# Fourteen modulation vectors of a two-model transformer kernel formed on VectorE instead of TensorE

## The chip, the cores and the metric

The kernel runs on one core of a Trainium2 chip. The metric is the device time of one execution in microseconds; the figure to be predicted is the median of several runs.

## The reference

Two small transformer models are evaluated one after the other on 256 tokens of width 1024 (the second model on 256 tokens and 256 context tokens). Each sub-layer normalises the residual stream, scales and shifts it, applies a mixer or a gated feed-forward network, and adds the result back under a gate. What matters here is where scale, shift and gate come from:

```python
mod = (jax.nn.silu(c) @ ada_w[layer] + ada_b[layer]).reshape(B, 3, 3, D)
h = modulate_pre(x, g[0, 0], mod[:, 0, 0], mod[:, 0, 1])
y = swiglu_ffn(h, ffn_w_in[layer, 0], ffn_w_out[layer, 0])
x = gated_post_add(x, y, g[0, 1], mod[:, 0, 2], 0.5)
...
shift, scale = jnp.split(jax.nn.silu(c) @ kv_ada_w + kv_ada_b, 2, axis=-1)
```

Each of these vectors is one product of a conditioning vector of 1024 numbers with a 1024 x 1024 block of a weight matrix: 4 MB of fp32 are read and each is used once. There are 32 of them, in fp32 throughout.

## The kernel before, in words

**Sub-layers.** `subs` holds eleven sub-layers, in this order: 0 feed-forward, 1 short convolution, 2 feed-forward, 3 the shared keys and values ("kv"), 4 feed-forward, 5 sparse attention ("nsa"), 6 feed-forward, then 7 to 10 of the second model. The change concerns 0, 2 and 4. Between 56 and 271 us of the profile lies sub-layer 0, between 281 and 403 sub-layer 1, between 412 and 626 sub-layer 2, from 636 on kv, between 709 and 926 sub-layer 4, and between 935 and 1111 nsa.

**A feed-forward sub-layer** with 256 tokens has eleven up steps and eleven down steps. Every weight comes in units of 1 MB (128 x 2048 fp32) into `stage`, a ring of three. ScalarE rounds a unit to `w_hi` (L689), VectorE subtracts to get `w_lo` (L1074), both rings of three, and TensorE forms hi x hi, lo x hi and hi x lo. An up step j uses two units, each with 48 matmuls of 128x256 (L1653 to L1655), in two halves q of 24. A down step uses one unit in 24 matmuls of 128x512 (L1705), 12 for each of two token tiles. Up steps run as one straight block of three, a hardware loop over two more such blocks, and steps 9 and 10; down steps run as three straight steps, a loop over two blocks of three, and two more. In the last two down steps the order is tile 0 with both units, then tile 1 with both.

**Between two sub-layers** (`boundary`) VectorE first splits the next sub-layer's first unit (`split(nu)`), and then, tile after tile, updates the residual stream (`y_update`, L1134, L1143) and normalises it (`x_norm`, up to L1157); TensorE transposes each tile (L1664), VectorE applies scale and shift (L1169), ScalarE and GpSimd split the result. TensorE's next matmuls wait for that.

**A modulation vector on TensorE.** Its 4 MB come in four units into `ada`, a ring of two, on the same in-order queue (SyncE's) as the weights. `vec_acc` (L1628) takes two of the units: 16 matmuls, with the conditioning column as the stationary operand and 512 columns of the unit moving; after both halves VectorE copies the row (`vec_row`, L1087), `vec_sum` (L1639, 4 matmuls that stand as 8 records) turns it into a column form, and `vec_col` (L1100) adds the bias. The semaphores `ada_used`, `ada_rowed`, `ada_sum` and `ada_col` count units, rows, sums and columns. In a feed-forward sub-layer each block of three up steps makes one vector (a half ahead of its first step, a half ahead of its second, the sum at its end), steps 9 and 10 and the first down step make two more: five for each of sub-layers 0, 2 and 4. The first half of the first vector of sub-layers 1 and 2 is placed into the boundary ahead of them (`fills`). In nsa five vectors are made in ten halves, at every second one of its jobs J = 2, 4 ... 20 (`nsa_vec`), among the attention's matmuls.

## Time and profile before

| | |
|---|---|
| median of three runs | 2375.61 us (2375.02 to 2376.76) |
| the profiled execution, its own time | 2372.45 us |
| its span in the trace | 2370.4 us |
| TensorE busy | 2208.2 us, 93% |
| VectorE busy | 1173.6 us, 50% |
| ScalarE busy | 931.5 us, 39% |
| GpSimd busy | 99.8 us, 4% |
| read from HBM | 408.47 MB, 173 GB/s over the span |

PE is TensorE's matmul row and PEld its weight loads, which overlap; DVE is VectorE, ACT ScalarE, POOL GpSimd. Matmuls are pipelined: the duration of one (0.28 us for 256 columns) is longer than the distance from one start to the next, and it is the distance that counts. An fp32 matmul stands as several records.

### The profile page before, as it was taken

The numbers are of one execution on the slowest core, as the hardware profiler recorded it, in microseconds if no ns is written. First come the engines' busy times: TensorE is split into PE (matmuls) and PEld (weight loads), VectorE is DVE, ScalarE is ACT, GpSimd is POOL, SyncE is SP. The second block draws the span as 40 slices with busy tenths as digits, with TensorE's granted clock in tenths as the row PEclk, the third lists the DMA queues.
The fourth block names the chain that finished last, engine by engine and source line by source line (L and its number), as shares of the span: only waits on it lengthen the run. The fifth ranks groups of instructions, "written<-read, shape, count | busy, mean of one in ns | idle before, by whom it ended". The sixth has DMA issues, their size and how long they took to land.

```text
span 2370.4 us, 35346 instructions
## 1 busy us (share of the span) xinstructions
PE 2208.2 (93%) x14350; PEld 1886.1 (80%) x14350; DVE 1173.6 (50%) x1973; ACT 931.5 (39%) x1376; POOL 99.8 (4%) x156
## 2 busy tenths in 40 slices
PE   4999998999889998998999899888999999898999
PEld 1898786998788977766998898566778768777997
DVE  2444556444634446464445663865222233865454
ACT  2333424333533335444335543654222122554343
POOL 2000000000100000011000100001000000200000
PEclk7999999999979999897999999999999999999999
DMA  7877686777548764651554422023435422215553
GB/s 270 277 256 266 221 302 243 244 253 267 166 146 275 265 253 142 225 203 54 196 178 156 132 78 88 1 72 106 156 112 177 176 91 98 89 54 184 173 178 124
DMA packets 246603, 411.41 MB, mean 174 GB/s; under 512 B 10221, under 2 KB 191942, under 8 KB 246470
## 3 DMA queue, kind: packets, MB, share of 16 engines
q1 hardware_dynamic: 246470, 409.54, 50.0%
q8 instruction: 95, 1.56, 0.3%
q14 instruction: 38, 0.31, 0.0%
HBM read 408.47 MB, written 1.05 MB: 173 GB/s over the span
## 4 chain that ended last, share of the span: by engine, by line
PE 82%; DVE 8%; DMA 4%; ACT 3%; issue 2%; POOL 1%; SPq 0%; DVEq 0%; ACTq 0%; POOLq 0%
PE bank L1705 20%; PE bank L1653 14%; PE bank L1654 13%; PE bank L1655 13%; PE bank L1628 5%; DMA ada<-in_ada_w 3%; PE bank L1762 3%; PE bank L1764 3%; PE bank L1763 3%; PE bank L1796 1%; PE bank L1639 1%; DVE astat L1444 1%; PE bank L1673 1%; PE bank L1883 1%; DVE w_lo L1074 1%
## 5 line engine op out<-in xcount | busy, mean ns | idle before, releaser
L1074 DVE TENSOR_TENSOR w_lo<-stage,w_hi 128x2048 fp32r<-128x2048 f32 x255 | 587.2, 2304 | 721.6 <-ACT w_hi L689 721.5
L1653 PE MATMUL bank<-h_hi,w_hi 128*128 128x256 f32 (+1 forms) x2432 | 740.7, 305 | 23.7 <-POOL h_lo L641 19.2
L1654 PE MATMUL bank<-h_lo,w_hi 128*128 128x256 f32 (+1 forms) x2432 | 732.2, 301 | 0.0
L1655 PE MATMUL bank<-h_hi,w_lo 128*128 128x256 f32 (+1 forms) x2432 | 731.8, 301 | 0.0
L689 ACT CAST w_hi<-stage 128x2048 fp32r<-128x2048 f32 x255 | 484.7, 1902 | 607.2 <-PE bank L1655 261.7
L1653 PEld LDWEIGHTS bank<-h_hi,w_hi 128*128 128x128 f32 x2432 | 472.1, 194 | 76.4 <-issue 61.5
L1654 PEld LDWEIGHTS bank<-h_lo,w_hi 128*128 128x128 f32 x2432 | 472.4, 194 | 14.7 <-issue 1.2
L1655 PEld LDWEIGHTS bank<-h_hi,w_lo 128*128 128x128 f32 x2432 | 471.7, 194 | 14.0
L1705 PE MATMUL bank<-w_hi,h_hi 128*128 128x512 f32 x776 | 246.7, 395 | 11.4 <-DVE h_lo L1083 9.2
L1705 PE MATMUL bank<-w_lo,h_hi 128*128 128x512 f32 x776 | 244.1, 392 | 0.0
L1705 PE MATMUL bank<-w_hi,h_lo 128*128 128x512 f32 x776 | 244.0, 392 | 0.0
L1705 PEld LDWEIGHTS bank<-w_hi,h_hi 128*128 128x128 f32 x776 | 145.3, 190 | 49.2 <-issue 14.6
L1022 ACT ACTIVATE silu_t<-bank 128x256 f32<-128x256 f32 (+1 forms) x132 | 54.9, 419 | 324.7 <-PE bank L1655 324.7
L1705 PEld LDWEIGHTS bank<-w_lo,h_hi 128*128 128x128 f32 x776 | 146.9, 189 | 31.1
L1705 PEld LDWEIGHTS bank<-w_hi,h_lo 128*128 128x128 f32 x776 | 146.8, 189 | 31.0
L1762 PE MATMUL bank<-w_hi,h_hi 128*128 128x256 f32 (+1 forms) x560 | 162.7, 291 | 8.8 <-issue 8.0
L1764 PE MATMUL bank<-w_hi,h_lo 128*128 128x256 f32 (+1 forms) x560 | 160.9, 287 | 0.0
L1763 PE MATMUL bank<-w_lo,h_hi 128*128 128x256 f32 (+1 forms) x560 | 160.8, 287 | 0.0
L1628 PE MATMUL bank<-ada,cond 128*32 128x512 f32 x1024 | 134.1, 634 | 21.6 <-DMA ada<-in_ada_w 20.9
L1528 DVE TENSOR_TENSOR mid<-silu_t,bank 128x256 f32 (+3 forms) x132 | 60.8, 463 | 119.4 <-PE bank L1655 119.4
L1762 PEld LDWEIGHTS bank<-w_hi,h_hi 128*128 128x128 f32 x560 | 110.4, 197 | 10.4 <-issue 9.3
L1764 PEld LDWEIGHTS bank<-w_hi,h_lo 128*128 128x128 f32 x560 | 110.3, 197 | 0.0
(205 smaller groups left out, 1870.9 us busy)
## 6 DMA issues: line engine op xcount, KB each, us to landing
ada<-in_ada_w SPq DMA_DIRECT2D x120, 1024.0 KB, 7.0
stage<-in_ffn_w_in SPq DMA_DIRECT2D x88, 1024.0 KB, 5.4
stage<-in_ffn_w_out SPq DMA_DIRECT2D x44, 1024.0 KB, 5.1
stage<-in_ffn_w_gu SPq DMA_DIRECT2D x44, 1024.0 KB, 5.1
stage<-in_ffn_w_down SPq DMA_DIRECT2D x22, 1024.0 KB, 4.9
stage<-in_a_w_in SPq DMA_DIRECT2D x12, 1024.0 KB, 7.8
stage<-in_diff_w_in SPq DMA_DIRECT2D x12, 1024.0 KB, 5.1
ada<-in_kv_ada_w SPq DMA_DIRECT2D x8, 1024.0 KB, 7.7
```

Source lines behind the costliest of these rows:

```text
L689: a.copy(w_hi[:, s, :], stage[:, s, :]).then_inc(hi_done, 1)
L1022: a.activation(silu_t[:, q, 0:T], bank[q][:, 0:T], ACT.Silu).then_inc(silu_done, 1)
L1074: v.tensor_tensor(w_lo[:, s, :], stage[:, s, :], w_hi[:, s, :].bitcast(F32), ALU.subtract).then_inc(lo_done, 1)
L1528: v.tensor_tensor(mid[:, bass.ds(o, T)], silu_t[:, q, 0:T], bank[2 + q][:, 0:T], ALU.mult).then_inc(mid_done, 1)
L1628: ins = m.matmul(bank[z0][z:z + 32, :], cond[:, b, 2 * q + k, :], ada[:, s, k * D + h * 512:k * D + (h + 1) * 512], start=(q == 0), stop=( ...
L1653: m.matmul(dst[:, 0:T], wh, h_hi[:, h0:h0 + T], start=(k == ks[0]), stop=False)
L1654: m.matmul(dst[:, 0:T], wh, h_lo[:, h0:h0 + T], start=False, stop=False)
L1655: ins = m.matmul(dst[:, 0:T], wl, h_hi[:, h0:h0 + T], start=False, stop=(k == ks[-1]))
L1705: ins = m.matmul(y_bank(T, tt, h)[:, :], a_[:, r:r + P], w_[:, slot, kc * D + h * 512:kc * D + (h + 1) * 512], start=first and n == 0, sto ...
L1762: m.matmul(dst, h_hi[:, r], w_hi[:, slot, c], start=(k == ks[0]), stop=False)
L1763: m.matmul(dst, h_hi[:, r], w_lo[:, slot, c], start=False, stop=False)
L1764: ins = m.matmul(dst, h_lo[:, r], w_hi[:, slot, c], start=False, stop=(k == ks[-1]))
```

## The change

In sub-layers 0, 2 and 4 (`dv`) vectors are accumulated on VectorE. `acc` is a tile of 128 x 1024 (the second half of `gate_b`). For each of the eight 128 x 1024 halves of the four units, VectorE multiplies by the conditioning number of the partition and adds to `acc` (the first one only multiplies); each of these waits for the one before by the semaphore `acc_s`. TensorE then sums `acc` over the partitions with `acc_sum`: eight matmuls, each with a 128 x 128 block of `acc` stationary and four columns of ones moving, which gives the column form at once; `acc_col` adds the bias. Four multiply-adds stand in each of two up steps of a block, between the two `split`s of that step; `acc_sum` stands in the next block, after the first half of its first unit. The fourth vector of a sub-layer is accumulated in up steps 9 and 10 and the first two down steps and summed after down step 2, the fifth in down steps 4 to 9 and summed ahead of the last 12 matmuls. Sub-layer 4 has four vectors instead of five, and nsa six instead of five, still on TensorE, at J = 22 and 24 in addition. So 5 + 5 + 4 = 14 vectors change engine. The second half of a vector is loaded with the third up step of a block instead of the second; a slot of `ada` is given back by `acc_s` instead of `ada_used`. The down steps of the three sub-layers are written out instead of looped. `fills` no longer holds for sub-layer 2.

```diff
-            if s["bsteps"] == FC // 2:
+            if s["bsteps"] == FC // 2 and not s["dv"]:
...
-        nsa_vec = {2 + 2 * n: (n // 2, n % 2) for n in range(10)}
+        nsa_vec = {2 + 2 * n: (n // 2, n % 2) for n in range(12)}
...
+        acc = gate_b[:, 1, :]
...
-                            if k < 2 and has_vec(s, i):
-                                load_vec(s["v"], src, j0, k, i)
+                            if k != (1 if s["dv"] else 2) and has_vec(s, i):
+                                load_vec(s["v"], src, j0, min(k, 1), i)
...
+            def acc_ops(vi, ks, i=None):
+
+                for kk in ks:
+                    q, k = kk // 2, kk % 2
+                    n = rv(vi) * VEC_UNITS + q
+                    w = ada[:, n % ADA_RING, k * D:(k + 1) * D]
+                    if k == 0 or kk == ks[0]:
+                        dve.wait_ge(ada_landed[n % ADA_RING], 16 * (n // ADA_RING + 1) + (0 if i is None else i * (16 * VEC_UNITS // ADA_RING)))
+                    if kk == 0:
+                        dve.wait_ge(ada_sum, rv(vi) + (0 if i is None else i))
+                        ins = v.tensor_scalar(acc, w, cond[:, 0, kk, 0:1], None, ALU.mult)
+                    else:
+                        dve.wait_ge(acc_s, acc_base(vi) + kk + (0 if i is None else i * 8))
+                        ins = v.scalar_tensor_tensor(out=acc, in0=w, scalar=cond[:, 0, kk, 0:1], in1=acc, op0=ALU.mult, op1=ALU.add)
+                    ins.then_inc(acc_s, 1)
+
+            def acc_col(vi, z, i=None):
+
+                dve.wait_ge(ada_sum, rv(vi) + (1 if i is None else i))
...
+                v.tensor_tensor(dst, src, b, ALU.add).then_inc(ada_col, 1)
...
                     def step(j, i=None):
                         split(u + 2 * j + 2, i, 6)
+                        if s["dv"]:
+                            if j == 9 or j == 0 and i is not None:
+                                acc_col(s["v"] + (2 if j else 0), 5, i)
+                            if j == 9:
+                                acc_ops(s["v"] + 3, range(0, 4))
+                            elif j < 2:
+                                acc_ops(s["v"], range(4 * j, 4 * j + 4), i)
                         split(u + 2 * j + 3, i, 6)
...
+                            if j == 10:
+                                acc_ops(s["v"] + 3, range(4, 6))
...
+                    if s["dv"]:
+                        if j < 2:
+                            acc_ops(s["v"] + 3, (6 + j,))
+                        if j == 3:
+                            acc_col(s["v"] + 3, 2)
+                        if s["nvec"] == 5 and j in last_acc:
+                            acc_ops(s["v"] + 4, last_acc[j])
+                last_acc = {4: (0, 1), 5: (2,), 6: (3,), 8: (4, 5), 9: (6, 7)}
                 for_b(dve, s, turn_over)
+                if s["dv"] and s["nvec"] == 5:
+                    acc_col(s["v"] + 4, 2)
...
+            def acc_sum(vi, z, i=None):
+
+                pe.wait_ge(acc_s, acc_base(vi) + (8 if i is None else i * 8))
+                pe.wait_ge(ada_col, rv(vi) + (0 if i is None else i - 1))
+                for c in range(KC):
+                    ins = m.matmul(bank[z][:, 4 * c:4 * c + 4], acc[:, c * P:(c + 1) * P], ones[:, 0:4], start=True, stop=True)
+                ins.then_inc(ada_sum, 1)
...
+                if s["dv"]:
+                    for j in range(2, nb - 2):
+                        step(j, None)
+                        if j == 2:
+                            pe.wait_ge(mid_done, s["c"] + 2 * nb)
+                            acc_sum(s["v"] + 3, 2)
...
+                        if last and s["dv"] and s["nvec"] == 5:
+                            acc_sum(s["v"] + 4, 2)
                         ins = products(j, None, tt, (0, 1), ((0,), (1,)) if last else ((0, 1),))
...
-                return s is not None and s["n"] > 0 and s["nvec"] > 0 and s["xb"] == 0 and s["kind"] != "nsa"
+                return s is not None and s["n"] > 0 and s["nvec"] > 0 and s["xb"] == 0 and s["kind"] != "nsa" and not s["dv"]
...
+                            if s["dv"] and j == 0 and i is not None:
+                                also = {(0, 0): (lambda: acc_sum(s["v"], 5, i),)}
```

## Rows read from the trace of the kernel before

**Rows 1.** The page: the chain that ended last, by engine.

```profile
PE 82%; DVE 8%; DMA 4%; ACT 3%; issue 2%; POOL 1%; SPq 0%; DVEq 0%; ACTq 0%; POOLq 0%
```

**Rows 2.** Timeline of PE in a block of sub-layer 0: start us, us, line.

```profile
96.28 0.28 PE L1655 MATMUL bank<-h_hi,w_lo 128*128 128x256 f32 x1
96.41 0.95 PE L1639 MATMUL bank<-sel,ada_row 128*128 128x4 f32 x8
97.29 1.92 PE L1628 MATMUL bank<-ada,cond 128*32 128x512 f32 x16
99.14 0.39 PE L1653 MATMUL bank<-h_hi,w_hi 128*128 128x256 f32 x1
...
110.64 0.28 PE L1655 MATMUL bank<-h_hi,w_lo 128*128 128x256 f32 x1
...
112.70 0.39 PE L1653 MATMUL bank<-h_hi,w_hi 128*128 128x256 f32 x1
```

**Rows 3.** Windows, L1628 alone: window, its us, PE busy, PEld busy, clock, DMA.

```profile
56.00:271.50 215.50, 19.24 (x160) 4.17 (x160) 0.99 0.75 264
708.00:925.60 217.60, 19.68 (x160) 4.10 (x160) 0.98 0.73 254
935.00:1082.00 147.00, 23.82 (x160) 3.81 (x160) 0.87 0.52 181
```

**Rows 4.** The first of these windows, L1639 alone.

```profile
56.00:271.50 215.50, 4.74 (x40) 4.96 (x40) 0.99 0.75 264
```

**Rows 5.** Lines by form: busy us, mean ns of one, idle before.

```profile
L1074 DVE TENSOR_TENSOR w_lo<-stage,w_hi 128x2048 fp32r<-128x2048 f32 x255 | 587.2, 2304 | 721.6 <-ACT w_hi L689 721.5
L1157 DVE TENSOR_SCALAR mid<-xs,norm_s 128x512 f32<-128x512 f32 x26 | 12.7, 488 | 0.9
L1458 DVE SCALAR_TENSOR_TENSOR mid<-mid,astat 128x512 f32<-128x512 f32 x16 | 12.0, 751 | 0.6
L1458 DVE SCALAR_TENSOR_TENSOR mid<-mid,astat 128x256 f32<-128x256 f32 x16 | 7.7, 484 | 0.6
```

**Rows 6.** Timeline of DVE in the convolution: operations that wait for each other.

```profile
299.82 0.48 DVE L1577 SCALAR_TENSOR_TENSOR silu_t<-mid,cols,silu_t 128x256 f32<-128x256 f32 x1
300.33 0.48 DVE L1579 SCALAR_TENSOR_TENSOR silu_t<-mid,cols,silu_t 128x256 f32<-128x256 f32 x1
```

**Rows 7.** Timeline of DVE in the same block as rows 2.

```profile
107.40 2.29 DVE L1074 TENSOR_TENSOR w_lo<-stage,w_hi 128x2048 fp32r<-128x2048 f32 x1 [6.57 <-ACT w_hi L689]
```

**Rows 8.** Windows, all: PE, PEld, DVE, ACT, POOL busy, clock, DMA share, GB/s.

```profile
99.14:110.64 11.50, 11.50 (x100) 11.50 (x96) 4.31 (x3) 2.56 (x3) 0.00 (x0) 1.00 1.00 346
96.28:135.71 39.43, 39.43 (x330) 36.41 (x329) 16.86 (x15) 13.37 (x12) 0.00 (x0) 1.00 0.77 268
```

**Rows 9.** The page's DMA issues: the ada units, us from issue to landing.

```profile
ada<-in_ada_w SPq DMA_DIRECT2D x120, 1024.0 KB, 7.0
```

**Rows 10.** Timeline of PE around the end of sub-layer 0.

```profile
268.56 0.39 PE L1705 MATMUL bank<-w_hi,h_hi 128*128 128x512 f32 x1
...
271.05 0.39 PE L1705 MATMUL bank<-w_hi,h_lo 128*128 128x512 f32 x1
```

**Rows 11.** Timeline of DVE around the end of sub-layer 0.

```profile
262.59 2.29 DVE L1074 TENSOR_TENSOR w_lo<-stage,w_hi 128x2048 fp32r<-128x2048 f32 x1 [2.52 <-ACT w_hi L689]
266.60 0.69 DVE L1134 TENSOR_TENSOR mid<-bank,gate_b 128x512 f32<-128x512 f32 x1 [1.71 <-ACT silu_t L723]
270.84 0.49 DVE L1157 TENSOR_SCALAR mid<-xs,norm_s 128x512 f32<-128x512 f32 x1
```

**Rows 12.** Timeline of PE in the boundary ahead of sub-layer 2.

```profile
404.20 1.93 PE L1628 MATMUL bank<-ada,cond 128*32 128x512 f32 x16
408.87 1.09 PE L1664 MATMUL bank<-ident,mid 128*128 128x128 f32 x8 [2.75 <-DVE mid L1157]
```

**Rows 13.** Windows, all: the end of nsa, and the boundary ahead of kv.

```profile
1060.00:1082.00 22.00, 16.89 (x91) 14.70 (x92) 9.37 (x37) 8.75 (x19) 2.89 (x4) 0.64 0.00 0
626.00:636.00 10.00, 3.54 (x19) 2.58 (x17) 8.88 (x26) 6.83 (x19) 3.18 (x4) 0.67 0.00 0
```

More of the change, by code:

```diff
@@ L107, in trace @@
         ada_col = sem("ada_col")
+        acc_s = sem("acc_s")
         part_done = [sem(f"part_done{i}") for i in range(3)]
@@ L155, in rv, with made_by_dve, rowed, ring_free @@
             return v if v < CMP_AT else v + 1
+        def made_by_dve(m):
+            return [v for s in subs if s["dv"] for v in range(s["v"], s["v"] + s["nvec"]) if rv(v) < m]
+        def rowed(m):
+            return m + 1 - len(made_by_dve(m))
+        def ring_free(n):
+            m = n // VEC_UNITS
+            v = m if m < CMP_AT else m - 1
+            if m != CMP_AT and v in made_by_dve(m + 1):
+                return acc_s, 8 * len(made_by_dve(m)) + 2 * (n % VEC_UNITS) + 2
+            return ada_used, n + 1 - VEC_UNITS * len(made_by_dve(m))
+        def acc_base(v):
+            return 8 * len(made_by_dve(rv(v)))
         def bias_col(v):
@@ L186, in add @@
             s = dict(n=len(subs), kind=kind, Td=Td or T, hb=hb, slots=slots, A=1 if len(subs) == 4 else 0, xb=0 if T == 256 and len(subs) not in (3, 4) else 4, cs=(1, 0) if kind == "diff" else (0, 1),
-                     ks=[3, 4, 5, 6, 7, 0, 1, 2] if kind == "diff" else list(range(KC)), w_in=w_in, w_out=w_out, T=T, v=N["vec"], nvec=nvec, v0=v0, u=N["unit"], c=N["chunk"],
+                     ks=[3, 4, 5, 6, 7, 0, 1, 2] if kind == "diff" else list(range(KC)), w_in=w_in, w_out=w_out, T=T, v=N["vec"], nvec=nvec, v0=v0, dv=len(subs) in (0, 2, 4), u=N["unit"], c=N["chunk"],
                      b=N["bstep"], sc=N["silu"], sb=list(N["step"]), g_pre=g_pre, g_post=g_post, weight=weight,
@@ L205, in trace @@
         add("kv", io["kv_w"], None, 256, 0, 9, col_at["kv_norm_g"], None, one, 6, 1, 0)
-        add("ffn", io["ffn_w_in"][1, 0], io["ffn_w_out"][1, 0], 256, 5, 11, norm_col(1, 0, 0), norm_col(1, 0, 1), half, 11, 2, 11)
-        add("nsa", io["b_w_in"][0], io["b_w_out"][0], 256, 5, 14, norm_col(1, 1, 0), norm_col(1, 1, 1), one, 5, 1, 4)
+        add("ffn", io["ffn_w_in"][1, 0], io["ffn_w_out"][1, 0], 256, 4, 11, norm_col(1, 0, 0), norm_col(1, 0, 1), half, 11, 2, 11)
+        add("nsa", io["b_w_in"][0], io["b_w_out"][0], 256, 6, 14, norm_col(1, 1, 0), norm_col(1, 1, 1), one, 5, 1, 4)
         add("ffn", io["ffn_w_in"][1, 1], io["ffn_w_out"][1, 1], 256, 0, 17, norm_col(1, 2, 0), norm_col(1, 2, 1), half, 11, 2, 11)
@@ L247, in has_vec @@
         def has_vec(s, i):
-            return s["nvec"] == 5 or s["nvec"] == 1 and i is None
+            return s["dv"] or s["nvec"] == 5 or s["nvec"] == 1 and i is None
         def unit_part(s, tag, n, q):
@@ L463, in load_vec @@
                     if n >= ADA_RING or i is not None:
-                        sp.wait_ge(ada_used, n - ADA_RING + 1 + (0 if i is None else i * VEC_UNITS))
+                        back = ring_free(n - ADA_RING + (0 if i is None else VEC_UNITS))
+                        per = 8 if back[0] is acc_s else VEC_UNITS
+                        sp.wait_ge(back[0], back[1] if i is None else back[1] - per + i * per)
                     c0 = j * D if i is None else i * D + j * D
@@ L536, in one_unit @@
                         single_vec(None)
+                    if s["dv"] and j == 1:
+                        load_vec(s["v"] + 3, *ada_src(s["v"] + 3), 1)
+                    if s["dv"] and s["nvec"] == 5 and j in (6, 10):
+                        load_vec(s["v"] + 4, *ada_src(s["v"] + 4), j // 10)
                 for_b(sp, s, one_unit)
@@ L559, in _ @@
                         load_unit(u + 2 * k + 1, col_unit(s["w_in"], FF + k * WCOL), KC)
-                        if s["nvec"] == 5:
+                        if s["dv"] and k == 9:
+                            load_vec(s["v"] + 3, *ada_src(s["v"] + 3), 0)
+                        elif s["nvec"] == 5 and not s["dv"]:
                             single_vec(s["v"] + k - 6)
@@ L1532, in block3 @@
                             step(j, i)
-                            if j == 1 and has_vec(s, i):
+                            if j == 1 and has_vec(s, i) and not s["dv"]:
                                 vec_row(s["v"], i)
-                        if has_vec(s, i):
+                        if has_vec(s, i) and not s["dv"]:
                             vec_col(s["v"], i)
@@ L1683, in down @@
                 if vec is None:
-                    pe.wait_ge(ada_col, rv(s["v"] + s["nvec"] - 1) + 1)
+                    pe.wait_ge(ada_col, rv(s["v"] + (2 if s["dv"] else s["nvec"] - 1)) + 1)
                 if s["kind"] in ("ffn", "conv"):
@@ L2038, in block3 @@
                             first = i is None and j == 0
-                            if j < 2 and has_vec(s, i) and not first:
+                            if j < 2 and has_vec(s, i) and not first and not s["dv"]:
                                 vec_acc(s["v"], j, i)
-                            up_step(j, i, 2, (0, 2), first,
-                                    {(0, 0): (lambda: vec_acc(s["v"], 0),)} if first and s["nvec"] and not fills(s) else None)
-                        if has_vec(s, i):
+                            also = None
+                            if s["dv"] and j == 0 and i is not None:
+                                also = {(0, 0): (lambda: acc_sum(s["v"], 5, i),)}
+                            elif first and s["nvec"] and not fills(s) and not s["dv"]:
+                                also = {(0, 0): (lambda: vec_acc(s["v"], 0),)}
+                            up_step(j, i, 2, (0, 2), first, also)
+                        if has_vec(s, i) and not s["dv"]:
                             vec_sum(s["v"], i)
@@ L2047, in _ @@
                     also = {}
-                    if s["nvec"] == 5:
+                    own = s["nvec"] == 5 and not s["dv"]
+                    if own:
                         vec_acc(v9, 0)
-                    up_step(9, None, 2, (0, 2), False)
-                    if s["nvec"] == 5:
+                    up_step(9, None, 2, (0, 2), False, {(0, 0): (lambda: acc_sum(s["v"] + 2, 5),)} if s["dv"] else None)
+                    if own:
                         vec_acc(v9, 1)
@@ L2056, in _ @@
                     up_step(10, None, 2, (0, 2), False, also)
-                    if s["nvec"] == 5 and not early:
+                    if own and not early:
                         vec_acc(v10, 1)
@@ L2086, in after @@
                         turn(nxt, tt - 2)
-                down(s, tag, s["v"] + 4 if early and s["nvec"] == 5 else None, after, nxt)
+                down(s, tag, s["v"] + 4 if early and s["nvec"] == 5 and not s["dv"] else None, after, nxt)
                 if nxt:
```

21 lines of the change are left out of this document (14 added, 7 removed).

## The prediction

> **What bounds the kernel.** I read the chain of waits first, to see which engine's time is the kernel's time: 82% of the span lies on TensorE [rows 1]. So an instruction removed there is worth its length wherever TensorE has no gap around it, and nothing where it fills one. The timeline of TensorE in a block of three up steps shows which it is: the last matmul of a block starts at 96.28, sum and half vector follow, weights resume at 99.14, and no row has an idle time [rows 2]. From 99.14 to 110.64 stand 96 starts, a distance of 0.121 us, so an up step is 11.6 us and a block without its vector 34.8 us. The windows say the same: TensorE is busy in all 39.43 us of the block, VectorE in 16.86, and the DMA share is 0.77 [rows 8]. VectorE has the room; its odd unit's subtraction began after 6.57 us of idleness [rows 7]. The transfers are no bound yet: in one up step the engines moved 346 GB/s at a share of 1.00 [rows 8], at which the 10 MB of a block (six weight units, four ada units, 10.5 million bytes) take 30.3 us.
>
> **Removed from TensorE.** In the 215 us of sub-layer 0 the halves cost 19.24 us [rows 3] and the sums 4.74 [rows 4], 24.0 us for five vectors, 4.8 each. This agrees with the timeline: 110.64 to 112.70 less one distance is 1.94 for a half, and 96.28 to 99.14 less one is 2.74 for a sum and a half [rows 2]: 4.7. Sub-layer 2 shows the same, but the first half of its first vector stands in the boundary at 404.20, and TensorE waits after it anyway until 408.87 with 2.75 us idle [rows 12]: 1.9 of its 24.0 us are worth nothing, 22.1 count. In sub-layer 4 the halves cost 19.68 [rows 3], and I add nothing for the waits between them: 24.4. Sum: 70.5 us.
>
> **Added to TensorE.** An `acc_sum` is eight matmuls of the form of which a `vec_sum` has four. Those eight records take 0.95 us, 0.10 a record with some 0.15 at the ends [rows 2]; sixteen take 1.75. Bounds: 0.95, were the length set by the ends alone, and 1.9, twice the row. Twelve stand in the open (four in each sub-layer): 21.0 us. The other two belong to the boundaries.
>
> **Added to VectorE.** Multiply-adds of two sources take 0.484 us for 256 columns and 0.751 for 512 [rows 5], 1.04 ns a column, so 1.285 for 1024. They wait for each other: two such in the convolution start 0.51 apart at a length of 0.48 [rows 6], so 1.31 each. The plain multiplication took 0.488 for 512 [rows 5]; for 1024 I take 0.76 (bounds: 0.49 and twice that). A vector is 0.76 + 7 x 1.31 = 9.9 us, all fourteen 139 us, less about 1 us a vector for the row copy and a second bias addition. What hides it is the slack of the odd unit. With time 0 at the start of an up step j, ScalarE rounds unit 2j+2 in 0 to 2.0, VectorE subtracts until 4.3 (2.29 each [rows 7]). In a looped block's first step `acc_col` waits for the sum (2.9 + 1.75, then the semaphore: 4.9); four operations run until 9.6. Unit 2j+3 is rounded from 5.8 on and subtracted at 9.6 to 11.9. TensorE wants it in the middle of the next step, at 17.4 or later: 5.5 us of slack, and the even unit is not touched. VectorE's sum per step is 4.6 for the two splits, 5.2, at most 1.0 for the two products of 256 columns (0.484 is the longest row of that width [rows 5]) and 0.2: 11.0 of 11.6 us, in two steps of three. Were the slack gone, each us more would stall TensorE by one.
>
> **The loads.** They wait on the in-order SyncE queue for slots that VectorE now frees. With the first step of a block as 0, the first half's slots come free at 6.9 and 9.5, during step 0; the second half's loads go out then (they follow the third step's weights, which go out at 4.3 of the same step), and are wanted at 17.7 and 20.3 (step 1 starts at 13.3): 10.8 us for a transfer of median 7.0 [rows 9]. The next vector's first half goes out in step 1 and has more than a step and a half. The weight unit behind them is due 11 us after its slot is free. The new block of 36.5 us needs 10.5 MB / 36.5 = 287 GB/s, 0.83 of what [rows 8] show.
>
> **The down steps.** A step is 24 matmuls at 0.227 (268.56 to 271.05 are twelve starts [rows 10]): 5.45 us. VectorE needs 2.3 + 0.7 us and now 1.3 to 2.6 more; unit j+2 is ready one step ahead. The tightest place is down step 1: operations 4 and 5 of the fourth vector stand between step 10 and the split it needs, which I find ready 1.6 us ahead. Writing the loop out I cost at nothing: all time of the chain that hangs on issue, loops included, is 2% [rows 1], and the pause of a loop's branch lies in TensorE's queue behind matmuls that still run.
>
> **The two boundaries.** Here the change adds a wait. After sub-layers 0 and 2 VectorE waits in `acc_col` for a sum that stands ahead of TensorE's last 12 matmuls. Behind it on VectorE are `split(nu)` (2.29) and the update of tile 0, for which the transposes, and so the next sub-layer, wait. Before, the split was over at 264.9 and tile 0 began at 266.60, under tile 1's matmuls [rows 11]. Now the sum begins at about 268.45 (the twelve matmuls' first start of 268.56 is where it goes in [rows 10]), its last record starts 1.6 later, VectorE adds the bias at 270.35, and after that and a small operation splits from 270.65 to 272.95: tile 0 begins 6.3 us later. Its chain to 270.84 + 0.49 was followed at once by tile 1's, so the whole boundary moves by 6.3, of which the sum itself is 1.75. Two of them: 12.6 us. Bounds: 2 x 1.75, were tile 1's matmuls the only bound, and 2 x 8.
>
> The Trainium skill, "TensorE: Matmul & The Clock Gate", Part 1, says that the clock falls to 1.2 GHz when the engine idles and comes back only after sustained work. Rows agree so far: 626 to 636, where it idles in a boundary, has a granted clock of 0.67, thus part of it at 1.2 GHz and part at 2.4 [rows 13]. That boundary is already cold when the next matmuls begin, so 4.5 us more of idleness cost nothing further in my sum; if the return is later too, it is the second rival.
>
> **The sixth vector in nsa.** Five cost 23.82 us there in halves alone [rows 3], so a sixth on full work would be 4.8 plus its sum, some 5.7. But it stands at J = 22 and 24, where TensorE is busy for only 16.89 of 22 us at a clock of 0.64 [rows 13]. Its last two units cannot be requested before J = 22 is used at about 1060, land 7 us later, and hold up TensorE to about 1070, 4.6 us behind; the rest then runs without its own waits and probably at the full clock. Bounds 0 and 9 (5.7 plus half of a 7 us landing); I take 3, nearer to the idle window.
>
> **The sum.** 70.5 - 21.0 - 12.6 - 3 = 33.9 us. The profiled execution of 2372.45 (its span of 2370.4 plus 2.05 around it) becomes 2338.6; the median is 3.16 above it, so 2341.7.
>
> **The rivals.**
> (1) *nsa pays in full.* The sixth vector costs 9 instead of 3: 2348. For it: the halves in nsa wait for transfers now. Against: no work follows that its end would hold up. Chance 0.10.
> (2) *The boundaries cost more*, because the clock returns later: 3 us more in each of two, 2348. For it the row of 0.67. The skill's rule just cited would say so. Chance 0.10.
> (3) *The sums and nsa are cheaper* (1.2 us a sum, nsa nothing because its end stays warm): 12 x 0.55 + 3 = 9.6 less, 2332. Chance 0.07.
> (4) *VectorE cannot take it: slower.* If a multiply-add of 1024 columns runs at x us instead of 1.31, a block on VectorE takes 6 x 2.29 + 3 x 1.0 + 0.5 + 8x; beyond x = 2.77 that is more than 39.43 and the kernel is slower. At x = 3.5 a block takes 45.2, 5.8 more in nine blocks, 52 us, and something in the tails: about 2430. A transfer that takes 19 us instead of 7 does the same, through the same wait in front of the odd unit's split. Against both: [rows 5, 9]. Chance 0.04.
> (5) *Nothing comes of it*: TensorE stalls at each step by the margins that I have as slack, or the boundaries eat it; 2372 to 2378. Against it: 5.5 us. Chance 0.03.
> The forecast has 0.66.
>
> **The range.** The forecast alone 2335 to 2348 (nsa 0 to 6, boundaries 2 us either way). Rivals 1 and 2 belong to it, and half of rival 3: 2332 to 2353, which leaves out some 0.18. What a measurement of this kernel can tell from no change is 0.2%, 4.8 us. Faster by more: 0.93; within: 0.03; slower: 0.04.
>
> **What would show it.** Blocks of sub-layers 0, 2, 4 of 36.5 us instead of 39.43, TensorE busy throughout; a multiply-add of 1.29 and 11 us of work in two of three up steps; no idle time of TensorE before an odd unit in an up step. After sub-layers 0 and 2 tile 0's update starting 6 us after the position it had, and TensorE's pause there 4 to 5 us longer; after sub-layer 4 no change. In nsa a wait for `ada` at J = 24. Wrong would be: operations much longer than 1.3, TensorE idle on `w_lo` or `h_lo` in down step 1, or waits of VectorE for `ada` in the blocks.

## The result, and the profile after

The changed kernel took 2339.93 us (median of four runs, 2337.01 to 2343.05), against 2376.19 for the kernel before beside it: a ratio of 0.9852 (95% interval 0.983 to 0.9874). A second set of five runs gave 2341.0 and 0.9838 (0.982 to 0.9856). The forecast was 2341.7. The profiled execution took 2337.01 with a span of 2335.0; its sum was forecast at 2338.6.

From the page after: first the engines' busy time, then the chain that ended last, the group of the new multiply-adds, and the landing time of the ada units.

```profile
PE 2168.2 (93%) x14014; PEld 1887.3 (81%) x14014; DVE 1292.1 (55%) x2057; ACT 932.8 (40%) x1376; POOL 103.9 (4%) x156
...
PE 81%; DVE 8%; DMA 4%; ACT 3%; POOL 2%; issue 2%; SPq 0%; DVEq 0%; ACTq 0%; POOLq 0%
...
L1146 DVE SCALAR_TENSOR_TENSOR gate_b<-ada,cond,gate_b 128x1024 f32<-128x1024 f32 x98 | 125.7, 1283 | 3.2
...
ada<-in_ada_w SPq DMA_DIRECT2D x120, 1024.0 KB, 6.3
```

TensorE's busy time fell by 40.0 us (before 2208.2), VectorE's rose by 118.5 (before 1173.6), and the chain is still TensorE's [rows 1]. Now the windows after: a block of sub-layer 0, the answer to the second line of [rows 8]; the two boundaries from the last down matmul; and the stretch of sub-layer 8 that is told of at the end.

```profile
93.75:130.09 36.34, 36.34 (x306) 36.34 (x305) 25.66 (x22) 13.38 (x12) 0.00 (x0) 1.00 0.83 290
253.42:267.62 14.20, 6.65 (x35) 3.06 (x33) 12.09 (x34) 8.91 (x25) 3.06 (x4) 0.71 0.22 76
600.00:614.20 14.20, 4.30 (x18) 3.13 (x16) 12.14 (x35) 8.88 (x24) 3.00 (x4) 0.64 0.22 74
1595.19:1996.98 401.79, 395.64 (x1808) 312.40 (x1808) 123.64 (x123) 97.44 (x93) 8.78 (x7) 0.98 0.39 135
```

The block takes 36.34 us instead of 39.43, with TensorE busy in all of it and VectorE in 25.66 instead of 16.86. The timeline of DVE in that block shows the order of an up step: even split, multiply-adds, odd split, products.

```profile
93.01 2.29 DVE L1104 TENSOR_TENSOR w_lo<-stage,w_hi 128x2048 fp32r<-128x2048 f32 x1 [1.44 <-ACT w_hi L719]
95.88 0.17 DVE L1158 TENSOR_TENSOR modv<-bank,cols 128x8 f32 x1 [0.58 <-PE bank L1724]
96.07 0.75 DVE L1143 TENSOR_SCALAR gate_b<-ada,cond 128x1024 f32<-128x1024 f32 x1
96.86 3.93 DVE L1146 SCALAR_TENSOR_TENSOR gate_b<-ada,cond,gate_b 128x1024 f32<-128x1024 f32 x3
100.82 2.29 DVE L1104 TENSOR_TENSOR w_lo<-stage,w_hi 128x2048 fp32r<-128x2048 f32 x1
...
108.52 5.24 DVE L1146 SCALAR_TENSOR_TENSOR gate_b<-ada,cond,gate_b 128x1024 f32<-128x1024 f32 x4
113.67 2.29 DVE L1104 TENSOR_TENSOR w_lo<-stage,w_hi 128x2048 fp32r<-128x2048 f32 x1
115.88 0.74 DVE L1592 TENSOR_TENSOR mid<-silu_t,bank 128x256 f32 x2
```

**Stage by stage.** The stages run between starts of matmuls in the timelines of PE: a sub-layer from its first up to its last down matmul, a boundary from there to the next first matmul. The forecast's column is the prediction's terms put into these stages; the fifth sum stands ahead of the last 12 matmuls and so in the sub-layer. The other three boundaries among these sub-layers take 9.85 to 9.86 us in both kernels and are left out.

| stage | before | after | change | forecast |
|---|---|---|---|---|
| start to first up matmul | 56.46 | 54.91 | -1.55 | 0 |
| sub-layer 0 | 214.59 | 198.51 | -16.08 | -15.25 |
| boundary 0 to 1 | 9.84 | 14.20 | +4.36 | +4.55 |
| convolution | 121.94 | 122.73 | +0.79 | 0 |
| sub-layer 2 | 213.32 | 199.78 | -13.54 | -13.35 |
| boundary 2 to kv | 9.87 | 14.27 | +4.40 | +4.55 |
| kv and sub-layer 4 | 289.37 | 270.81 | -18.56 | -17.4 |
| nsa | 176.32 | 178.11 | +1.79 | +3 |
| sub-layer 6 to the last down matmul | 1243.74 | 1246.64 | +2.90 | 0 |

### The profile page after: what moved, and what is told of

It reads as the page before. It is cut to its first block, busy times and chain, and to the rows that moved or that the text cites. A ratio compares the mean times of both kernels' runs of the same rounds, so it can differ in the third digit from the quotient of the medians.

```text
span 2335.0 us, 34631 instructions
## 1 busy us (share of the span) xinstructions
PE 2168.2 (93%) x14014; PEld 1887.3 (81%) x14014; DVE 1292.1 (55%) x2057; ACT 932.8 (40%) x1376; POOL 103.9 (4%) x156
## 4 chain that ended last, share of the span: by engine, by line
PE 81%; DVE 8%; DMA 4%; ACT 3%; POOL 2%; issue 2%; SPq 0%; DVEq 0%; ACTq 0%; POOLq 0%
PE bank L1790 20%; PE bank L1738 14%; PE bank L1739 14%; PE bank L1740 14%; DMA ada<-in_ada_w 3%; PE bank L1705 3%; PE bank L1855 3%; PE bank L1857 3%; PE bank L1856 3%; PE bank L1889 1%; DVE w_lo L1104 1%; PE bank L1724 1%; PE bank L1758 1%; DVE astat L1501 1%; PE bank L1976 1%
## 5 line engine op out<-in xcount | busy, mean ns | idle before, releaser
L1790 PEld LDWEIGHTS bank<-w_lo,h_hi 128*128 128x128 f32 x776 | 146.9, 189 | 30.9
L1790 PEld LDWEIGHTS bank<-w_hi,h_lo 128*128 128x128 f32 x776 | 146.9, 189 | 30.9
L1146 DVE SCALAR_TENSOR_TENSOR gate_b<-ada,cond,gate_b 128x1024 f32<-128x1024 f32 x98 | 125.7, 1283 | 3.2
L1856 PEld LDWEIGHTS bank<-w_lo,h_hi 128*128 128x128 f32 x560 | 109.9, 196 | 0.0
```

What stands on the lines that cost most here:

```text
L1146: ins = v.scalar_tensor_tensor(out=acc, in0=w, scalar=cond[:, 0, kk, 0:1], in1=acc, op0=ALU.mult, op1=ALU.add)
L1790: ins = m.matmul(y_bank(T, tt, h)[:, :], a_[:, r:r + P], w_[:, slot, kc * D + h * 512:kc * D + (h + 1) * 512], start=first and n == 0, sto ...
L1856: m.matmul(dst, h_hi[:, r], w_lo[:, slot, c], start=False, stop=False)
```

## The experiments

Each kernel is the changed one with a small edit; all ran beside the kernel before. "Median" is that of the kernel's runs in us, "ratio" that to the kernel before with its 95% interval; the other columns are stages of the profiled execution in us. "Sum in boundary" and "nsa light" do not compute what the reference does: the one overwrites a part of its transposes, the other leaves matmuls out.

| kernel | median us | ratio (95%) | sub-layer 0 | boundary | sub-layer 2 | boundary | kv and 4 | nsa |
|---|---|---|---|---|---|---|---|---|
| changed, again | 2341.0 | 0.9838 (0.982 to 0.9856) | 198.50 | 14.19 | 199.32 | 14.27 | 270.84 | 181.03 |
| column late | 2329.28 | 0.9791 (0.9771 to 0.9812) | 199.50 | 9.17 | 199.68 | 9.17 | 272.09 | 178.10 |
| column late, again | 2328.11 | 0.9766 (0.9742 to 0.979) | 198.78 | 9.17 | 199.44 | 9.17 | 271.90 | 181.33 |
| sum in boundary | 2328.2 | 0.979 (0.9773 to 0.9807) | 197.84 | 10.56 | 197.56 | 10.63 | 272.10 | 178.24 |
| the same, two banks | 2323.52 | 0.9762 (0.9742 to 0.9781) | 197.74 | 10.55 | 197.55 | 10.63 | 272.10 | 168.53 |
| after both splits | 2335.53 | 0.9817 (0.9803 to 0.9831) | 198.61 | 14.19 | 199.44 | 14.29 | 270.83 | 174.46 |
| before both splits | 2370.37 | 0.9967 (0.9952 to 0.9981) | 209.95 | 14.19 | 212.61 | 14.26 | 278.40 | 177.24 |
| loads early | 2343.39 | 0.986 (0.984 to 0.988) | 204.77 | 14.20 | 202.22 | 14.28 | 271.68 | 173.33 |
| one more each | 2368.78 | 0.9955 (0.9937 to 0.9973) | 207.98 | 14.20 | 213.56 | 14.29 | 280.59 | 174.26 |
| two more each | 2498.17 | 1.0502 (1.0486 to 1.0519) | 255.94 | 12.64 | 255.05 | 14.33 | 316.21 | 182.17 |
| two sub-layers | 2357.41 | 0.9911 (0.9898 to 0.9925) | 198.71 | 14.20 | 199.42 | 14.27 | 289.09 | 181.89 |
| nsa light | 2332.04 | 0.9818 (0.98 to 0.9836) | 199.32 | 14.20 | 199.30 | 14.28 | 270.84 | 170.44 |

Read the stages that an edit touches, not the totals alone: nsa moves by more than most effects here, with the same instructions in it.

**1. The fifth vector's bias addition late.**

```diff
                 for_b(dve, s, turn_over)
-                if s["dv"] and s["nvec"] == 5:
-                    acc_col(s["v"] + 4, 2)
...
                         x_norm(s, tt, one[0:4] if tt == 1 else ())
+                        if tt == 0 and prev["dv"] and prev["nvec"] == 5:
+                            acc_col(prev["v"] + 4, 2)
```

> The bias addition of the fifth vector after sub-layers 0 and 2 moves behind tile 0's update and normalisation, so VectorE no longer waits for the sum before its split. Theory (the wait of VectorE in front of the split delays tile 0 and so the transposes): both boundaries, 14.2 and 14.3 us from the last down matmul to the next sub-layer's first, go back to about 9.85, 8.8 us in all, and the kernel to about 2331. The start of the convolution, 0.8 us slower after the change, gains that back too if it came from the longer idle time. Rival (the sum on TensorE itself, or the clock, makes the boundary longer): they stay at 14 or fall by at most 1.75 each, 2336 to 2340.

Both boundaries fell from 14.2 to 9.17 us, 10.1 in all; kv and sub-layer 4 gave back 1.3 (of it 0.7 in kv's first 144 matmuls, 19.46 us instead of 18.75), so 8.9 us of stages. The two pairs of profiled executions are 7.8 and 6.8 us apart in span (2335.0 and 2327.2, 2338.9 and 2332.1), and the medians fell by 11 to 13; what they fell by more than the stages is not put down to the edit. The boundaries end 0.7 us below the 9.84 of the kernel before, not at 9.85 as was expected. The timeline of DVE after sub-layer 0 in the changed kernel:

```profile
250.96 0.17 DVE L1158 TENSOR_TENSOR modv<-bank,cols 128x8 f32<-128x8 f32 x1 [5.36 <-PE bank L1724]
251.05 0.16 DVE L1165 SCALAR_TENSOR_TENSOR modc<-modv,cols 128x8 f32<-128x8 f32 x1
251.12 2.29 DVE L1104 TENSOR_TENSOR w_lo<-stage,w_hi 128x2048 fp32r<-128x2048 f32 x1
253.32 0.68 DVE L1191 TENSOR_TENSOR mid<-bank,gate_b 128x512 f32<-128x512 f32 x1
```

and with the late addition, where the last down matmul starts at 254.97:

```profile
247.15 2.28 DVE L1104 TENSOR_TENSOR w_lo<-stage,w_hi 128x2048 fp32r<-128x2048 f32 x1
249.35 0.68 DVE L1191 TENSOR_TENSOR mid<-bank,gate_b 128x512 f32<-128x512 f32 x1
...
253.99 0.16 DVE L1158 TENSOR_TENSOR modv<-bank,cols 128x8 f32<-128x8 f32 x1
```

In the first VectorE stands still for 5.36 us ahead of an addition of 0.17, and tile 0's update starts 0.10 before the last down matmul (253.32 against 253.42). In the second it starts 5.62 before it, in the kernel before 4.45 [rows 10, 11]. The wait was VectorE's, not TensorE's, and neither the sum nor the clock made the boundary long: the sum still stands where it stood. This version beats the kernel before and the changed one. It ran a second time:

> The kernel with the late bias addition once more, unaltered, to compare its ratio with the first and with that of the other kernel in this call. Theory: a ratio within 0.977 to 0.981, boundaries of 9.17 us again, and nsa somewhere between 173 and 182 us. Rival (its first result was one of the shorter spells): 0.982 or more.

The ratio of 0.9766 lies just below the span that was named, and its interval overlaps the first one's; the boundaries are 9.17 again.

**2. The sum in the boundary.** From the kernel of 1:

```diff
-                        if last and s["dv"] and s["nvec"] == 5:
-                            acc_sum(s["v"] + 4, 2)
...
                     turn(nxt, n_tiles - 2)
+                    if s["dv"] and s["nvec"] == 5:
+                        acc_sum(s["v"] + 4, 5)
```

> As the kernel with the late bias addition, and now the sum of the fifth vector itself, 1.84 us of TensorE ahead of the last 12 down matmuls, stands behind tile 0's transposes, where TensorE had 2.2 us of idleness in front of tile 1's transposes; the bias addition follows tile 1's normalisation. Theory: the last down matmuls start 1.7 us sooner. In the kernel with the late bias addition VectorE waited 0.82 and 0.40 us for ScalarE in tile 1's update and ScalarE 0.52 for those matmuls, so not all 1.7 come through: 1.0 to 1.7 us less in each of two sub-layer ends, 2 to 3.4 in all, and about 2327. Rival (TensorE's work ahead of the last matmuls is hidden by VectorE's chain of tile 0 by now): no change, 2329.

After sub-layer 2 the sum in this kernel overwrites part of tile 0's transposes in bank 5. In both versions the bias addition moves on behind tile 1's normalisation, and TensorE waits for it after tile 1's transposes. The second version takes bank 2 there:

> The kernel with the fifth vector's sum behind tile 0's transposes, now with the sum in bank 5 after sub-layer 0 and in bank 2 after sub-layer 2, so that no transpose is overwritten. In the kernel before it the last down matmuls started 1.7 us sooner, but the boundaries grew from 9.17 to 10.56 and 10.63, as VectorE's chain of tile 0 by then sets tile 1's start. Theory (that chain bounds it, whatever the bank): sub-layer and boundary together 0.3 to 0.6 us less than with the late bias addition alone, no difference that a run can tell. Rival (the one bank held something up after sub-layer 2): 1 us or more less there.

The sub-layers lost 1.0 to 2.1 us, the boundaries gained 1.4 to 1.5. Sub-layer and boundary together stand at 208.2 to 208.4 us against 208.0 to 208.9 with the late addition alone. So the first expectation failed, its rival (no change) holds, and the second expectation, at most half a us, holds too. Tile 1's update follows tile 0's normalisation and ScalarE's two passes behind it, whenever the matmuls end. Timeline of DVE there:

```profile
252.75 0.49 DVE L1214 TENSOR_SCALAR mid<-xs,norm_s 128x512 f32<-128x512 f32 x1
254.13 0.69 DVE L1191 TENSOR_TENSOR mid<-bank,gate_b 128x512 f32<-128x512 f32 x1 [0.90 <-ACT silu_t L753]
```

So what is left of the boundary belongs to the chain of VectorE and ScalarE, and at its end GpSimd: TensorE's last wait there is 2.76 us, for `h_lo`. The lower median of the second version stands beside nsa's 168.5 us and is not put down to the edit.

**3. The place of the multiply-adds.** The edit for the place behind both splits; ahead of both, the even split moves behind the multiply-adds instead.

```diff
                         split(u + 2 * j + 2, i, 6)
+                        split(u + 2 * j + 3, i, 6)
                         if s["dv"]:
...
-                        split(u + 2 * j + 3, i, 6)
```

> The multiply-adds of an up step stand behind both subtractions instead of between them. The place between them was costed at nothing, since the odd unit has 5.5 us of slack. Theory (slack on either side): a block stays at 36.3 us, the kernel within 0.2% of 2340; the products of the step begin up to 5 us later and are wanted only by the next down part or the next use of the banks. Rival (the place matters, as the row of slots freed later, the second half's loads, or the products hold something up): a block above 37, nine of them 6 us or more.

> The multiply-adds of an up step stand ahead of both subtractions. In the first step of a looped block they wait for the sum until 4.9 us after the step's start, run until 9.6, and the even unit is then ready at 11.9 instead of 4.3, when TensorE wants it at 11.6; the odd one at 14.2, wanted at 17.4. Theory (slack ends near the step's length): a block gets about 0.3 to 1.5 us longer by a stall ahead of the even unit, six or so looped blocks, so 2 to 13 us: about 2346. Rival (no slack counted by place, since only VectorE's sum counts): a block of 36.3 and 2340. Rival (every us behind the old place counts): 7.6 us a block, about 2400.

Behind both splits the block takes 36.34 us, to the hundredth, and the three sub-layers agree within 0.4 us; the lower median comes with nsa's 174.5 us. Ahead of both splits a block takes 40.79: more than expected. Its windows (the block from the end of one sum to the end of the next, then 6 us behind the stall), the stall in the timeline of PE, and DVE ahead of it:

```profile
97.70:138.49 40.79, 38.08 (x307) 37.88 (x306) 25.30 (x21) 13.39 (x12) 0.00 (x0) 0.96 0.72 250
120.80:126.80 6.00, 6.00 (x37) 6.00 (x38) 5.01 (x4) 0.41 (x2) 0.00 (x0) 0.72 0.79 278
```

```profile
120.80 0.39 PE L1738 MATMUL bank<-h_hi,w_hi 128*128 128x256 f32 x1 [2.71 <-DVE w_lo L1104]
```

```profile
113.30 5.25 DVE L1146 SCALAR_TENSOR_TENSOR gate_b<-ada,cond,gate_b 128x1024 f32<-128x1024 f32 x4 [5.20 <-DMA ada<-in_ada_w]
118.46 4.49 DVE L1104 TENSOR_TENSOR w_lo<-stage,w_hi 128x2048 fp32r<-128x2048 f32 x2
```

The sum that was expected left out the queue. The waits of SyncE's queue in that block, and below them those of the changed kernel's block:

```profile
SPq L475 <- DVE w_lo L1104: 32.8, 5, 12.7
```

```profile
SPq L475 <- DVE w_lo L1104: 21.8, 6, 5.4
SPq L492 <- DVE gate_b L1146: 8.3, 4, 2.2
```

A weight load waits up to 12.7 us for a split, and the ada loads stand behind it: they are issued at 106.02, 10.0 us after the block's sum has begun at 96.00, instead of 4.6 us after it (98.31 against 93.75). So the second four multiply-adds wait 5.20 us for data, and the splits wait behind them. The expected 2 to 13 us became 30 in the median. Of the 4.4 us by which the block is longer, 2.9 are the stall, and 1.5 lie behind it: 120 matmul starts in 15.85 us instead of 14.35, at a granted clock of 0.72 over 6 us, so partly at 1.2 GHz, after TensorE had been idle for 2.71.

**4. The loads of the second half early.**

```diff
-                            if k != (1 if s["dv"] else 2) and has_vec(s, i):
-                                load_vec(s["v"], src, j0, min(k, 1), i)
+                            if k < 2 and has_vec(s, i):
+                                load_vec(s["v"], src, j0, k, i)
```

> The second half vector's loads are issued in the second up step, as in the kernel before, and not in the third. They stand in SyncE's queue ahead of that step's successor's weights and wait there for slots that VectorE frees. Theory (the weights have 11 us of room and the transfers are below their bound, 290 GB/s against 346): the block stays at 36.3 us and the kernel within 0.2% of 2340. Rival (the place of the loads in the queue is a part of the gain, because the slots are freed only in the following block's first step): weights behind them come late, TensorE waits for stage or w_hi in each block, 1 to 5 us a block, 2349 to 2385.

By the total this is within the noise (0.986 against 0.9852 and 0.9838), but the stages say otherwise: sub-layers 0 and 2 are 6.3 and 2.4 us longer, kv and 4 0.9, and an nsa of 173.3 us hides it. The waits of SyncE's queue and the timeline of ACT in the first looped block:

```profile
SPq L492 <- DVE gate_b L1146: 16.3, 4, 10.3
SPq L475 <- DVE w_lo L1104: 11.2, 3, 7.3
```

```profile
113.99 1.90 ACT L719 CAST w_hi<-stage 128x2048 fp32r<-128x2048 f32 x1 [10.67 <-DMA stage<-in_ffn_w_in]
```

The early ada load waits up to 10.3 us for VectorE's multiply-adds, the weight loads stand behind it, ScalarE rounds late, and TensorE stops for 1.77 us until 126.05. Behind that:

```profile
126.05:136.12 10.07, 10.07 (x71) 10.07 (x72) 6.06 (x6) 4.37 (x4) 0.00 (x0) 0.83 0.82 283
```

The 72 starts to the block's end take 10.07 us instead of 8.58, at a granted clock of 0.83: a stop of 1.77 us was followed by a fall of the clock to 1.2 GHz, as one of 2.71 was in the run before, and cost almost its own length again. The next block had 34.91 us of up matmuls instead of 34.51. So the rival holds where it happens, in the first blocks, and the theory in the later ones.

**5. More of VectorE's work.**

```diff
                         dve.wait_ge(acc_s, acc_base(vi) + kk + (0 if i is None else i * 8))
+                        for r in range(EXTRA):
+                            v.scalar_tensor_tensor(out=acc, in0=w, scalar=cond[:, 0, kk, 1:2], in1=acc, op0=ALU.mult, op1=ALU.add).then_inc(dum_s, 1)
+                            dve.wait_ge(dum_s, ...)
```

> Ahead of each of the seven multiply-adds of a vector stands one more of the same form with a scalar of zero, so VectorE takes about 9.2 us more for each of the 14 vectors, 126 us in all (98 more of 1.285 us), and the sum of the output is the same. Theory (slack of the odd unit, then a stall of what goes beyond it): in a block's second step the odd unit's split ends some 2 us after TensorE wants it, so a block takes about 38, 1.5 more in nine blocks, and the three down parts some 2 us each: about 20 us more than the change, 2355 to 2360. Rival (all of VectorE's added work comes to light, no slack): 126 us more, 2465. Rival (5.5 us of slack in each step, none spent): 2340.

> Two more multiply-adds with a scalar of zero ahead of each of the seven, 18.3 us more of VectorE a vector, 252 us in all. Theory: VectorE is the bound of a block, 6 x 2.29 of splits, 28.1 us of vector and 3 of products, some 45.5 us against 36.3, 9.2 more in nine blocks is 83, and in the three down parts, where each step has 5.45 us, some 8 us each: 2440 to 2450, slower than before by 3%. The step from one extra operation to two must then cost far more (about 90) than the first (15 to 20). Rival (the loss is in proportion, each us of VectorE above what the change has costs the same): twice the loss of the kernel with one extra operation.

Windows of a looped block of sub-layer 0 with one more each, and with two; the third line is the stretch behind the second one's long stall.

```profile
97.99:135.87 37.88, 36.56 (x307) 36.38 (x306) 34.80 (x29) 13.37 (x12) 0.00 (x0) 1.00 0.83 278
```

```profile
108.16:156.84 48.68, 38.34 (x306) 37.99 (x305) 43.37 (x36) 13.31 (x12) 0.00 (x0) 0.89 0.64 215
146.59:156.72 10.13, 10.13 (x71) 10.13 (x72) 6.14 (x6) 4.35 (x4) 0.00 (x0) 0.83 1.07 362
```

With one more each the looped block is 37.88, as worked out (38), for 9.2 us more of VectorE's work. The first blocks (2.8 and 4.8 us longer) and what follows the third block's sum, the down part above all (3.6 and 5.5, where 2 were expected) brought the sum to 33 us of stages and the median to 28 above the changed kernel, not 20. With two more each the loss is 158 us: the step from one to two costs 130, the first 28. That shape speaks for slack that is used up, but both sizes were too low. A block is 48.68, not 45.5, because VectorE is busy in only 43.37 of it: it waits in turn for the sum, for ScalarE and for TensorE's banks. TensorE's stalls are 1.3 and 9.0 us in the block, and behind the long one 72 starts take 10.13 us instead of 8.58. The waits of PE in the same two blocks name what is late:

```profile
PE bank L1743 <- DVE mid L1597: 1.3, 1, 1.3
```

```profile
PE bank L1743 <- DVE mid L1597: 10.3, 2, 9.0
```

It is the first product behind the odd split, which frees the bank that TensorE needs for the odd unit, and not the split itself. Behind the stall of 1.3 us with one more each the clock stayed at 1.00 and the last 72 starts took 8.58 us as without it; behind the 9.0 they cost 1.5 more.

**6. Two sub-layers only.**

```diff
-dv=len(subs) in (0, 2, 4)
+dv=len(subs) in (0, 2)
...
-        add("ffn", io["ffn_w_in"][1, 0], ..., 256, 4, 11, ...)
-        add("nsa", io["b_w_in"][0], ..., 256, 6, 14, ...)
+        add("ffn", io["ffn_w_in"][1, 0], ..., 256, 5, 11, ...)
+        add("nsa", io["b_w_in"][0], ..., 256, 5, 14, ...)
```

> Only sub-layers 0 and 2 have their vectors on VectorE; sub-layer 4 has its five and nsa its five on TensorE as in the kernel before. Theory (the gains are those of each sub-layer and add up): 24.0 + 22.1 - 8 x 1.75 - 12.6 = 19.5 us, by the stages of the trace 20.8, so about 2356 in the time of the run before of 2376; what is missing against the change is sub-layer 4's 18.8 less the 2 of nsa. nsa itself is then 176 us as before, not 178. Rival (nsa's sixth vector costs 9, the boundary after sub-layer 4 or the clock gives something back): the difference to the change is 8 to 10 us only.

2357.41 and 0.9911, 21 us of gain in the time of 2376. kv and sub-layer 4 are at 289.09, as before (289.37), and the others as in the changed kernel: the gains add up. What did not hold is nsa: with its old five vectors it took 181.89 us, where the kernel before took 176.32.

**7. nsa's sixth vector.**

```diff
                     for k in range(2):
                         for h in range(2):
+                            if vi == 25 and (k, h) != (1, 1):
+                                continue
```

> Of the matmuls of nsa's sixth vector 12 of 16 are left out; its loads, waits, row copy and sum stay, so the values of that vector are not the reference's. Theory (the sixth vector costs 2 to 3 us, of which most is the wait for its last transfer at J = 24, since it stands where TensorE waits anyway): the same as the change within 1.5 us. Rival (its work is what costs): 3 us less. nsa's duration differed by up to 4.8 us among runs with the same code of it (173.3 to 178.1 us), so the stage is read by its own timeline around J = 24 and not by the total alone.

nsa took 170.4 us, but 168.5 with the full vector in another run, so the total decides nothing. The vector's own places tell more. Timeline of PE at J = 24 in the changed kernel:

```profile
1027.40 1.06 PE L1705 MATMUL bank<-ada,cond 128*32 128x512 f32 x8
1030.63 1.87 PE L1705 MATMUL bank<-ada,cond 128*32 128x512 f32 x8 [2.17 <-DMA ada<-in_ada_w]
1032.43 1.92 PE L1961 MATMUL bank<-ident,diag 128*128 128x128 f32 x8
```

The expected wait for the last transfer is there, 2.17 us. In the light kernel it is 1.61, with a quarter of the matmuls:

```profile
1026.92 1.04 PE L1707 MATMUL bank<-ada,cond 128*32 128x512 f32 x2 [1.61 <-DMA ada<-in_ada_w]
```

What the vector is worth in nsa's length is left open.

**8. The changed kernel again.**

> The changed kernel once more, unaltered, beside the others. Two reasons are to be told apart for two differences without a cause in an edit: nsa took 178.1 us in its profile and 173.3 to 182.2 in those of seven other kernels with the same instructions there (or with one vector less), and the first four steps of the convolution took 18.7 to 19.7. If both hang on when TensorE's clock is granted in that execution, this run's profile will differ from the first one's too, by some us, at another granted clock, and its ratio lies within 0.982 to 0.987. If they belong to the kernel, nsa takes 178 us again and the convolution's first 144 matmuls 19.6.

nsa took 181.0 us against 178.1, the convolution's first 144 matmuls 19.58 against 19.59. So nsa varies without an edit; the convolution's start repeated here, but over thirteen profiles it took 18.5 to 19.7, with long boundaries and with short ones.

## Why the prediction was right

**TensorE's side.** Removed less the inline sums was right to 0.2 to 1.2 us in each of three sub-layers. A sum takes 1.71 us to the next matmul's start (93.75 to 95.46); 1.75 was taken. Sub-layer 4 gained 1.2 more than forecast, and 0.9 of that are waits that the step left out and the change removed: before, TensorE is idle for 0.89 us in it (0.6 for `ada`, 0.3 for a bias addition), after not at all. Writing out the down loop was costed at nothing and was not tried by itself; the agreement leaves it little room.

**VectorE's side.** 1.283 us a multiply-add, 0.75 the plain multiplication, next start 1.31 to 1.32 later: a vector is 9.9 to 10.0 us as forecast. The slack held: from its first up matmul to its last down matmul TensorE is never idle in sub-layer 0, so not in down step 1 either, the place that was called the tightest. That it is real and about as large as worked out (5.5 us) is shown by the block with the work behind both splits, whose product in the second step begins 3.8 us later (120.32 in a block from 94.37, against 115.88 in one from 93.75) at no cost, by the block with one more operation each, 1.54 us longer, and by the loss of 12.3 with two. Named wrongly was the object: TensorE waits for the product behind the odd split. In the changed kernel that product is over at 116.3 (115.88 + 0.41) and its bank is wanted at about 121.4 (95.46 and 216 starts): 5.1 us.

**The loads.** They landed in 6.3 us and held up nothing. Two runs show that this hangs on the order: both a split and an ada load that waits for VectorE hold up the one queue behind them.

**The boundaries.** 4.36 and 4.40 more from the last down matmul, against 4.55; the cause, VectorE waiting for the sum with the split and tile 0 behind it, is shown by removing it. As forecast, the boundary ahead of nsa did not change (9.85 and 9.86). Rival 2, a clock that returns later, did not add 3 us: kv's first 144 matmuls took 18.75 us where they had 18.85, and the convolution's 0.7 more than before, which other runs with the same boundary did not always show (18.54 to 19.70).

**nsa.** The wait at J = 24 came, at 2.17 us instead of the 4.6 that were worked out. The term of 3 us is neither shown nor refuted: the one profile gave 1.8, at a spread of 14 us.

**What the sum owes to chance.** The start-up's 1.55 less and the 2.9 more behind nsa were not in it. The start-up ran from 54.4 to 56.5 us over all profiles. Without both, the profile would stand 1.4 below where it does. The stages that the sum speaks of came out 3.7 us faster than forecast (the three sub-layers gained 2.2 more, nsa cost 1.2 and the boundaries 0.3 less), the convolution, at nothing in it, 0.8 slower. That the profile's total is off by only 1.6 is in part luck.

Rival 4, that VectorE cannot take the work, needed 2.77 us an operation and met 1.31. The run with two more each shows what it would have looked like: 5% slower.

## What to carry to other kernels

Work moved to an idle engine costs by its place: give it a place behind which the next consumer has slack, and count that slack for everything behind it, the products and the slots that a shared in-order queue waits for, not for the operation beside it alone. A short operation that waits for the bottleneck engine does not belong in front of that engine's next chain: here 0.17 us of addition cost 5 us at each of two places, and one later line gave them back. Where one stage scatters by more than the effect, compare the stages that the edit touches, across several profiles, before reading the total.

## What the hardware showed unexpectedly

**nsa's length goes with the granted clock.** Windows over the whole of nsa: the kernel with two banks, the changed one, the late addition again, and two sub-layers (one vector less).

```profile
887.61:1056.14 168.53, 156.06 (x1171) 119.63 (x1172) 89.26 (x374) 74.19 (x199) 14.02 (x20) 0.95 0.58 201
```

```profile
894.92:1073.03 178.11, 165.13 (x1171) 125.68 (x1172) 89.31 (x374) 74.31 (x199) 13.99 (x20) 0.89 0.55 191
```

```profile
888.93:1070.26 181.33, 170.11 (x1172) 129.39 (x1172) 89.41 (x374) 74.37 (x199) 13.99 (x20) 0.86 0.55 187
```

```profile
914.49:1096.38 181.89, 168.02 (x1132) 131.18 (x1132) 88.64 (x371) 74.21 (x199) 13.97 (x20) 0.85 0.47 164
```

The same instructions take 168.5 us at 0.95 and 181.3 at 0.86; a window with one vector less took 181.9 at 0.85. It is not the waits themselves that grow: TensorE is idle for 12.5 us in the first window and 11.2 in the third. The order is not strict either: the run ahead of both splits has 177.2 us at 0.91, the one behind both 174.5 at 0.90. So some executions spend more of nsa at 1.2 GHz than others; that its many short waits let this happen is a guess, and what decides it was not found.

**GpSimd and VectorE slow each other.** At the start of sub-layer 8 VectorE's first split meets GpSimd's last subtractions. Before, DVE and then POOL:

```profile
1635.39 4.74 DVE L1074 TENSOR_TENSOR w_lo<-stage,w_hi 128x2048 fp32r<-128x2048 f32 x1 [2.27 <-ACT w_hi L689]
```

```profile
1635.15 2.82 POOL L649 TENSOR_TENSOR h_lo<-mid,h_hi 128x256 fp32r<-128x256 f32 x4
```

and after, followed by TensorE's row:

```profile
1597.31 2.65 DVE L1104 TENSOR_TENSOR w_lo<-stage,w_hi 128x2048 fp32r<-128x2048 f32 x1 [2.27 <-ACT w_hi L719]
```

```profile
1597.08 6.89 POOL L679 TENSOR_TENSOR h_lo<-mid,h_hi 128x256 fp32r<-128x256 f32 x4
```

```profile
1604.03 0.50 PE L1738 MATMUL bank<-h_hi,w_hi 128*128 128x512 f32 x1 [1.17 <-POOL h_lo L679]
```

Before, the split took 4.74 us instead of 2.29 and GpSimd's four ran through in 2.82; after, the split took 2.65 and GpSimd's four 6.89, and TensorE waited for them. Sub-layer 8 is 401.79 us instead of 399.19, most of the 2.9 behind nsa, and nearly all of it arises within its first 22 matmuls. But the wait for GpSimd is only about half: the 21st matmul already starts 7.27 us after the first instead of 6.06, ahead of any wait, because the clock returned later. In the second 3 us of the sub-layer it stood at 0.57 (1598.19 to 1601.19) where it had stood at 1.00 (1636.27 to 1639.27). Of the contention, the untouched code gave this side in all thirteen profiles of changed kernels (GpSimd's last fourteen take 13.8 us in each), and the other in the one profile of the kernel before (9.70 us); that the change brings it about is therefore likely but not shown, and what would tip it was not tried. The Trainium skill, "GPSIMD Engine Reference", Specifications, says that GpSimd's paths to the on-chip memory are shared with VectorE and that instructions of VectorE with two inputs there contend for them. The rows agree: the split has two.
